# One level of Strassen's multiplication for the input projection of a short convolution, in token passes of 768, 768 and 640

## What is computed

```python
proj = rmsnorm(x, g) @ w_in                    # 2176 x 1024 times 1024 x 4096
b_gate, c_gate, h, z = split(proj, 4)          # four matrices of 1024 columns
u = c_gate * h
conv = w[0]*u[t-2] + w[1]*u[t-1] + w[2]*u[t]   # causal, three taps
y = silu(z) * b_gate * conv
x = x + rmsnorm(y @ w_out)                     # second stage, phase_out
```

## Time and profile before

| | |
|---|---|
| median of 3 runs | 2816.25 us (2815.89 to 2818.65) |
| the profiled execution, own time | 2820.25 us |
| its span in the trace | 2818.7 us |
| first matmul of the projection starts | 22.23 us |
| last matmul of the projection starts | 794.45 us |
| first matmul of phase_out starts | 797.31 us |
| matmuls of the projection | 3840 |
| busy share of PE, DVE, ACT, POOL over the span | 98%, 58%, 47%, 41% |

### The profile page before, as it was taken

How to read it: one execution, slowest core, us unless ns; L and a number is a source line. 1 busy time by engine, 2 the same in 40 slices (tenths; PEclk the granted TensorE clock), 3 DMA queues, 4 the chain that set the end, 5 groups by cost and what they waited for, 6 DMA issues and landing times. The chain is left out here.

```text
span 2818.7 us, 42045 instructions
## 1 busy us (share of the span) xinstructions
PE 2755.2 (98%) x14856; PEld 2409.4 (85%) x14856; DVE 1645.2 (58%) x2152; ACT 1315.5 (47%) x2733; POOL 1156.5 (41%) x1023
## 2 busy tenths in 40 slices
PE   7999999999999999999989999999999999979998
PEld 6999999999978888889978888888888888868886
DVE  5321232123244450102249999999999999998775
ACT  6000000000034441111148888888888888875543
POOL 3333333233210020002356877777777768651110
PEclk9999999999999999999999999999999999999999
DMA  5101110111064444424578676777777866766873
GB/s 160 38 24 38 38 38 22 38 38 38 9 202 131 136 152 153 174 102 157 166 219 269 197 245 198 237 215 217 223 222 207 251 203 207 224 184 203 239 229 107
DMA packets 280359, 433.33 MB, mean 154 GB/s; under 512 B 52578, under 2 KB 218594, under 8 KB 274180
## 3 DMA queue, kind: packets, MB, share of 16 engines
q1 hardware_dynamic: 269156, 391.41, 45.4%
q0 software_dynamic: 11040, 39.86, 4.7%
HBM read 307.40 MB, written 123.81 MB: 153 GB/s over the span
## 5 line engine op out<-in xcount | busy, mean ns | idle before, releaser
L1994 POOL TENSOR_TENSOR a_a<-a_a,a_prod 128x512 f32<-128x512 f32 (+3 forms) x640 | 661.1, 1051 | 270.3 <-DVE a_prod L1945 196.0
L1945 DVE TENSOR_TENSOR_SCAN a_prod<-a_keep,a_prod,a_restart 128x513 f32<-128x513 f32 x384 | 478.0, 1269 | 7.5 <-ACT a_keep L1889 5.7
L1888 ACT ACTIVATE a_a<-a_pz 128x512 f32<-128x512 f32 (+3 forms) x640 | 357.4, 559 | 69.4 <-PE a_pz L1815 44.4
L1955 DVE TENSOR_TENSOR a_atl<-a_pt,a_ath 128x512 fp32r<-128x512 f32 (+3 forms) x640 | 363.0, 599 | 33.0 <-ACT a_ath L1898 29.9
L1889 ACT ACTIVATE a_keep<-a_pz 128x512 f32<-128x512 f32 (+3 forms) x640 | 361.4, 565 | 0.0
L1898 ACT ACTIVATE a_ath<-a_pt 128x512 fp32r<-128x512 f32 (+3 forms) x640 | 333.0, 558 | 57.8 <-PE a_po L1829 34.2
L1838 PEld LDWEIGHTS a_pt<-ident_r,a_bits 128*128 128x128 f32 x2176 | 231.4, 141 | 51.1 <-DVE a_atl L1955 7.4
L285 POOL TENSOR_TENSOR w_wh<-w_raw,w_gain 128x1024 fp32r<-128x1024 f32 x22 | 41.7, 1897 | 534.2 <-PE v_pg L355 278.9
L1814 PE MATMUL a_pz<-a_kh,a_q 128*128 128x512 f32 (+3 forms) x640 | 246.9, 389 | 8.7 <-ACT a_keep L1889 6.2
L1827 PE MATMUL a_po<-a_ath,a_v 128*128 128x512 f32 (+3 forms) x640 | 250.8, 396 | 2.7 <-POOL a_v L2005 1.9
L1838 PE MATMUL a_pt<-ident_r,a_bits 128*128 128x128 f32 x2176 | 244.2, 241 | 6.4 <-DVE a_atl L1955 4.2
(11 more groups left out here) (234 smaller groups left out, 6128.0 us busy)
## 6 DMA issues: line engine op xcount, KB each, us to landing
a_x<-x_d SPq DMA_DIRECT2D x84, 896.0 KB, 6.7
a_x<-x_d SPq DMA_DIRECT2D x56, 832.0 KB, 5.9
a_kh<-kh_t SPq DMA_DIRECT2D x32, 512.0 KB, 6.9
a_kl<-kl_t SPq DMA_DIRECT2D x32, 512.0 KB, 8.8
w_raw<-in_a_w_in POOLq DMA_DIRECT2D x30, 512.0 KB, 4.8
x<-f_xn POOLq DMA_DIRECT2D x17, 512.0 KB, 5.9
g_y_in<-sz_t SPq DMA_DIRECT2D x17, 512.0 KB, 7.9
g_x<-x SPq DMA_DIRECT2D x17, 512.0 KB, 3.6
```

The costliest lines, as they stand in the source:

```text
L1888: act.activation(a[:, s, q, 0:w], pz[:, n % ZS, 0:w], ACT.Sigmoid, scale=SCALE)
L1945: dve.tensor_tensor_scan(prod[:, s, 0:w + 1][:, ::-1], keep[:, n % KS, 0:w + 1][:, ::-1], restart[:, 0:1].broadcast_to([P, w + 1]), prod[: ...
L1955: dve.tensor_tensor(atl[:, b % AS, c0:], pt[:, turn_slot(pr, hh, b), c0:], ath[:, b % AS, c0:].bitcast(F32), ALU.subtract).then_inc(at_spl ...
L1994: pool.tensor_tensor(part, part, prod[:, n % PS, after:after + w], ALU.mult).then_inc(weighted, 1)
```

## The change

Tokens go in three passes of 768, 768 and 640 (`PASSES` gives start and half width: 384, 384, 320). A strip is (pass, c, pair of matrices), 48 in all. Even strips (m = 0) make c_gate and h of one column c, odd strips (m = 1) z and b_gate. Within a strip the weights are a 2 x 2 block matrix A (which matrix x which half of the 1024 inputs) and x is a 2 x 2 block matrix B (which half of the inputs x which half of the pass's tokens). Seven products of 4 x 3 matmuls take the place of eight. Sums of weights S1 to S4 are made by POOL for each strip, differences of x T1 to T4 once a pass. Each of the seven weight operands is split by ACT (high) and DVE (low) anew for every strip, and each of the seven x operands once a pass. The gain is folded into x when DVE reads the transposes (`stage`). Norm and transposes of the tiles of passes 1 and 2 are spread over the strips of the pass before. Three PSUM banks a strip, two sets: bank A takes A11*B11 and, once ACT has copied it, A12*B21; bank B takes S1*T1 and S4*B22; bank C takes S2*T2, S3*T3 and A22*T4. DVE adds the partial results (v, u2, c12, c22, c21). Products with the gates move from DVE to POOL, the first tap and the carry of two tokens between passes move to ACT, the other taps stay with DVE. `phase_norm_in` goes; its work is in `phase_conv`. In phase_out, 5 of the 8 row blocks of w_out are split ahead of the barrier (4 high and 2 low before), and two scratch tiles lie elsewhere.

```diff
+PASSES = [(0, 384), (768, 384), (1536, 320)]
+STRIPS = [(p, c, m) for p in range(NPASS) for c in range(KT) for m in range(2)]
+FIRST_TILES = 2 * PASSES[0][1] // P
...
+            def product(n, i):                       # TensorE
+                w, fresh = width(n), i in (A11_B11, S1_T1, S2_T2)
...
+                elif i == A12_B21:
+                    pe.wait_ge(p1_read, n + 1)
+                elif i == S4_B22:
+                    pe.wait_ge(v_read, n + 1)
+                elif i == S3_T3:
+                    pe.wait_ge(u2_read, n + 1)
+                elif i == A22_T4:
+                    pe.wait_ge(c22_read, n + 1)
+                if first_of_pass(n):
+                    pe.wait_ge(x_lo[i], p + 1)
+                pe.wait_ge(w_lo[i], n + 1)
+                o = bank(n, b, w)
+                for k in range(NH):
+                    x_h, x_l = room.xh[i][:, k, 0:w], room.xl[i][:, k, 0:w]
+                    pe.matmul(o, room.wh[i][:, k, :], x_h, start=fresh and k == 0, ...)
+                    pe.matmul(o, room.wh[i][:, k, :], x_l, start=False, ...)
+                    mm = pe.matmul(o, room.wl[i][:, k, :], x_h, start=False, ...)
+            for t in range(FIRST_TILES):
+                turn(t)
+            for n in range(NSTRIP):
+                if n >= 2 and n - 2 in norm_of:
+                    turn(norm_of[n - 2])
...
+                product(n, A11_B11)
+                product(n, S1_T1)
+                if n:
+                    product(n - 1, A22_T4)
+                product(n, S2_T2)
+                product(n, A12_B21)
+                product(n, S4_B22)
+                product(n, S3_T3)
...
+            for n in range(NSTRIP):                  # ScalarE
+                act.wait_ge(done[A11_B11], n + 1)
+                act.activation(room.p1[:, n % 2, 0:w], bank(n, BANK_A, w), ACT.Copy).then_inc(p1_read, 1)
+                high(n + 1, A11_B11)
+                if m == 0 and n:
+                    open_gate(n - 1)
+                if m == 0:
+                    prefix(n)
+                high(n + 1, S1_T1)
+                high(n, A22_T4)
+                if m == 1:
+                    keep_and_tap(n)
+                high(n + 1, S2_T2)
+                act.wait_ge(done[A12_B21], n + 1)
...
+                high(n + 1, A12_B21)
+                high(n + 1, S4_B22)
+                high(n + 1, S3_T3)
+                if n in norm_of:
+                    sums_of(norm_of[n])
+                if n - 1 in norm_of:
+                    scale(norm_of[n - 1])
...
+            for n in range(NSTRIP):                  # VectorE
+                if n:
+                    c22(n - 1)
+                    low(n, S3_T3)
+                low(n + 1, A11_B11)
...
+                add(room.v[:, 0:w], n, BANK_B, room.p1[:, n % 2, 0:w], v_read)
+                low(n + 1, S1_T1)
+                if n:
+                    c21(n - 1)
+                low(n, A22_T4)
...
+                add(room.u2[:, 0:w], n, BANK_C, room.p1[:, n % 2, 0:w], u2_read)
+                low(n + 1, S2_T2)
+                if n % 2:
+                    taps(n)
+                low(n + 1, A12_B21)
+                if n - 2 in norm_of:
+                    stage(norm_of[n - 2])
...
+                    add(room.cg[:, w:2 * w], n, BANK_B, room.u2[:, 0:w], c12_read)
...
+                low(n + 1, S4_B22)
...
+            sums(0)                                  # GpSimd
+            first_differences(0)
+            third_difference(0)
+            for n in range(NSTRIP + 1):
+                if n and n % 2:
+                    set_u(n - 1, 1)
+                if n + 1 < NSTRIP:
+                    sums(n + 1)
+                if n and n % 2 == 0:
+                    gate(n - 1, 0)
+                    gate(n - 1, 1)
+                    finish(n - 1, 1)
+                if n % PER_PASS == PER_PASS - 2 and n < PER_PASS * (NPASS - 1):
+                    first_differences(n // PER_PASS + 1)
+                if n % PER_PASS == PER_PASS - 1 and n < PER_PASS * (NPASS - 1):
+                    second_difference(n // PER_PASS + 1)
+                if n and n % 2:
+                    set_u(n - 1, 0)
+                elif n:
+                    finish(n - 1, 0)
+                if n % PER_PASS == PER_PASS - 1 and n < PER_PASS * (NPASS - 1):
+                    third_difference(n // PER_PASS + 1)
```

More of the change, by code:

```diff
@@ L109, in make_tools @@
     return sb, pb, sem, sem2
[L112 to L256, removed]
@@ L361 @@
 EDGES_AT, BORDER_SIZE = 34336, 38432
[L362 removed]
+AHEAD = 5
 class Border:
@@ L428, in phase_conv @@
[L428 to L436 removed]
+        pc = pb("c_pc", [P, 6, 512])
@@ new lines, in phase_conv @@
+        t_set = sem2("c_t_set", 4)
+        raw_loaded = [sem2(f"c_raw_loaded_{x}") for x in "xy"]
+        summed = sem("c_summed")
+        w_hi, w_lo, x_hi, x_lo, done = sem7("w_hi"), sem7("w_lo"), sem7("x_hi"), sem7("x_lo"), sem7("done")
+        p1_read, c11_read, v_read, u2_read, c12_read, c22_read, c21_read = (
+            sem("c_read_" + n) for n in ("p1", "c11", "v", "u2", "c12", "c22", "c21"))
+        opened, prefixed, u_set, tapped, kept, gated = (
+            sem("c_" + n) for n in ("opened", "prefixed", "u_set", "tapped", "kept", "gated"))
@@ new lines, in phase_conv, with bank, width, first_of_pass @@
+        tail = SEQ - PASSES[-1][0]
+        def bank(n, b, w):
+            return pc[:, 3 * (n % 2) + b, 0:w]
+        def width(n):
+            return PASSES[STRIPS[n][0]][1]
+        def first_of_pass(n):
+            return n % PER_PASS == 0
+        def tiles_staged(p):
+            return 2 * (sum(tokens_of(p)[::2]) // P)
+        def pair(n):
+            return n // 2
+        def turned_at(t):
+            if t < FIRST_TILES and t % 2:
+                return pc[:, 4:6, :].rearrange("p b (k f) -> p (b k) f", f=P)
+            return pt[:, :, :]
@@ new lines, in _ @@
+            act.wait_ge(eps_set, 1)
+            act.activation(room.std[:, 0:1], epsb[:, :], ACT.Sqrt).then_inc(warm, 1)
+            act.wait_ge(warm, 1)
+            for t in range(FIRST_TILES):
+                sums_of(t)
+                if t:
+                    scale(t - 1)
+                if t == 3:
+                    high_w(0, A11_B11)
+                elif t == 4:
+                    high_x(0, A11_B11)
+            scale(FIRST_TILES - 1)
+            high_w(0, S1_T1)
+            high_x(0, S1_T1)
@@ L511, in _ @@
+            open_gate(LAST)
             act.wait_ge(e_turned, 1)
+            for i in (A11_B11, A12_B21, A22_T4):
+                act.wait_ge(w_lo[i], LAST)
+            act.wait_ge(summed, 4 * LAST)
             for half in range(2):
[L513 to L516 removed]
@@ L576, in begin_next, with inverse, stage @@
-            def begin_next(g):
-                if g == 1:
+            def inverse(t):
+                dve.wait_ge(std_ready, t + 1)
+                dve.reciprocal(room.rstd[:, t:t + 1], room.std[:, t:t + 1]).then_inc(rstd_ready, 1)
+            def stage(t):
+                p = next(p for p in range(NPASS) if t * P < sum(tokens_of(p)[::2]))
+                at = t * P - PASSES[p][0]
+                dve.wait_ge(turned, t + 1)
+                if t == 0:
+                    dve.wait_ge(gain_loaded, 16)
+                for h in range(2):
+                    half = slice(NH * h, NH * (h + 1))
+                    dve.tensor_tensor(room.stage[:, half, at:at + P], turned_at(t)[:, half, :],
+                                      gain[:, half].unsqueeze(2).broadcast_to([P, NH, P]), ALU.mult).then_inc(staged, 1)
@@ new lines, in add, with c22, c21 @@
+            def add(out, n, b, other, read):
+                w = width(n)
+                dve.tensor_tensor(out, bank(n, b, w), other, ALU.add).then_inc(read, 1)
+            def c22(n):
+                w = width(n)
+                dve.wait_ge(done[S3_T3], n + 1)
+                wait_past(dve, u_set if n % 2 else y_done, 2 * pair(n) + (1 if n % 2 else -1))
+                dve.wait_ge(v_read, n + 1)
+                add(room.sums[:, 1, 0:w], n, BANK_C, room.v[:, 0:w], c22_read)
+            def c21(n):
+                w = width(n)
+                dve.wait_ge(done[A22_T4], n + 1)
+                wait_past(dve, u_set if n % 2 else y_done, 2 * (pair(n) + n % 2))
+                add(room.sums[:, 0, 0:w], n, BANK_C, room.p1[:, n % 2, 0:w], c21_read)
@@ L580, in begin_next @@
                                       ALU.subtract).then_inc(border.y_lo, 1)
-                elif 2 <= g < 2 + LOW_AHEAD:
-                    border.low_weights(dve, range(g - 2, g - 1))
-            with dve.Fori(0, KT - 1) as c:
-                conv_and_gate(c)
-            conv_and_gate(KT - 1)
+                k = n - PER_PASS * (NPASS - 1) - 7
+                if 0 <= k < AHEAD:
+                    border.low_weights(dve, range(k, k + 1))
+            c22(LAST)
+            c21(LAST)
+        @block.gpsimd
```

645 lines of the change are left out of this document (449 added, 196 removed).

## The result

| | before | after |
|---|---|---|
| median | 2817.45 us, 4 runs (2815.89 to 2821.12) | 2859.02 us, 4 runs (2855.14 to 2862.51) |
| span of the profiled execution | 2818.7 | 2860.8 |
| first matmul of the projection starts | 22.23 | 25.6 |
| last matmul of the projection starts | 794.45 | 830.80 |
| first matmul of phase_out starts | 797.31 | 834.78 |

The ratio is 1.0145, with a 95% interval of 1.0128 to 1.0163: slower by 1.5%. The forecast was 2803 with a range up to 2855.

The account below looks back on a forecast made before the run. PE's matmul pace bounds the projection: 657.5 + 9.7 + 5 + 25 + 38 + 45 + 1.5 = 781.7 us against 794.6, 13 less, so a median of 2803 from 2816.25; range 2750 to 2855.

Parts of the forecast that it names:

- Eleven tiles' transposes stand between products, 0.64 a tile, with the switch 0.73: 8.0: Projection, on PE: eleven tiles' transposes between products add 8.0 us by their own duration and the switch.
- the whole term of 9.7: Work added on PE in the projection: 8.0 us for tile transposes, 1.7 for transposes of stream state and edges.
- 2 us of half pace, in the start: Start of the projection: 2 us for matmuls at half pace after idle, counted within the 45 us of start.
- c22 in passes 0 and 1: Steady strips of 384 columns: PE just doesn't wait for DVE's c22; 5 us in all for 16 pairs, 0 to 35.
- c22 late in every odd strip: Slower rival, 27%: POOL's set_u, ACT's keep_and_tap and DVE's S2 operand delay c22; 2874 us, half way 2840.
- sign for that rival: Passes 0 and 1: the slower case shows if PE waits over 1 us in each pair.
- Last pass and steps: PE's waits: 25 us in the last pass (5 to 54), 38 at the two steps between passes (25 to 50).
- 26.4 in 24.0: Last pass: operations of POOL and DVE that take turns need 26.4 us in a pair of strips of 24.0.
- a walk through the order of the queues: Last pass: following the engines' operations ends c22 at 17.6 to 18.7, needed at 15.5; 21 us over 8 pairs.
- The rival in which they cost as much as 384 columns: Matmuls of 320 columns: if the weight load sets 0.173 us each, 40 us more, 2843; chance 5%.
- Start: Start of the projection: 45 us beyond the products, against 36 before; between 37 and 50.
- turns as the forecast took them: A DVE operation with two SBUF inputs and a POOL operation take turns, each whole; one that waited costs 0.15 less.

Follow-up runs that it names:

- turn_late: Changed kernel with each tile's transposes moved from the strip's head to behind product A22*T4 of the strip before: 2824.16 us, ratio 1.0014 to the kernel before.
- keep_clock: Changed kernel with 22 transposes of the identity on PE ahead of the wait for the scaled tile: 2838.11 us, ratio 1.0069 to the kernel before.
- one_x: Changed kernel without the x operands of passes 1 and 2, the products using those of pass 0: 2819.51 us in one execution.
- u_mid: u_ahead with POOL's first half of u, in the last pass, between its second and third sum of the next strip: 2800.41 us, ratio 0.9932.
- u_ahead: turn_late plus DVE's taps in even strips, u2_first's order, and POOL's u product ahead of the second difference in strips 14 and 30: 2811.63 us, ratio 0.9971.
- u2_first: turn_late with DVE making u2 before the operands of A22*T4 in the first strip of each pass: 2822.15 us, ratio 1.0013.

## Why the prediction was wrong

**The step that failed: "Eleven tiles' transposes stand between products, 0.64 a tile, with the switch 0.73: 8.0".** It counts the instructions that PE gained and not what they wait for; for the wait the sum has nothing, and gives no reason. The transposes wait for ACT's scaling, the scaling stands behind the high part of the next S3 operand, and that waits for the end of the product just before the transposes. This can be read from the order of the calls in the changed kernel: PE waits at least for ACT's two operations, which take 0.54 and 1.13. The wait measured 1.76 each, 1.93 from start to start, 21.2 in all, with 11.7 of half pace behind it. turn_late shows it: without these waits the kernel is 35 us faster, 1.45% of slowdown becomes 0.14%, and the forecast's sum would have been off by 13 us instead of 50. The price of the transposes themselves was nearly right: the whole term of 9.7 measured 11.5.

**The second: the clock.** The forecast allowed 2 us of half pace, in the start. Yet a row showed it: 0.42 a matmul behind a wait of 2.52. The waits of PE that the forecast did count, 5, 25 and 38 us, carried none of it. It measured 36.7 us beside 95 us of waits. keep_clock shows that it is a cost of its own.

**c22 in passes 0 and 1: right, and better than taken.** 5 was the term, 0 was measured away from the step between them, also in turn_late, where no other wait can cover it. The rival "c22 late in every odd strip", whose times of 2840 to 2874 hold the measured one, is therefore not what happened: the time fell into its range by another cause. The forecast's sign for that rival was a wait of over 1 us in each pair of the first two passes. PE waited so in 13 of the 16: in eleven for the tile, in the two at the steps for u2 and c22.

**Last pass and steps: the waits were sized well.** 25 forecast and 25.3 measured, 38 and 31.3; the half pace, 10.8 and 6.0, comes on top. For the steps the work on the x operands is the reason, as forecast (one_x). For the last pass the forecast gave two reasons, the sum "26.4 in 24.0" and a walk through the order of the queues, and the trace bears out the walk. This is strip 41 of the changed kernel, ahead of a wait for c22; POOL, ACT, DVE, then PE:

```profile
734.91 0.89 POOL L865 TENSOR_TENSOR c_u<-c_sums,c_cg 128x320 f32<-128x320 f32 x1
```

```profile
735.82 0.20 ACT L592 ACTIVATE c_edge<-c_u 128x2 f32<-128x2 f32 x1 [4.40 <-POOL c_u L865]
```

```profile
737.60 0.69 DVE L699 TENSOR_TENSOR c_wl<-c_s,c_wh 128x512 fp32r<-128x512 f32 x1 [3.40 <-ACT c_wh L554]
```

```profile
745.51 0.64 PE L474 MATMUL c_pc<-c_xh,c_wh 128*128 128x320 f32 x1 [5.71 <-DVE c_sums L706]
```

DVE stands idle for 3.40 us in the strip whose c22 comes 5.71 too late: it waits for ACT, and ACT for the half of u that POOL makes behind four sums. So it isn't DVE's time that is short there, and u_mid, with all the work, wins 10 us by order alone. That the 25 of the forecast met the 25.3 doesn't show the sum of turns to be right.

**Matmuls.** 384 columns are 0.1733 as in the earlier trace rows. 320 columns are 0.1463 where 0.143 was taken, 0.002 above the higher of its two bounds; with it the matmuls are 4.9 us more. The rival in which they cost as much as 384 columns fell. These lines give 0.145 to 0.146 a start:

```profile
829.35 0.31 PE L475 MATMUL c_pc<-c_xl,c_wh 128*128 128x320 f32 x1
829.49 0.30 PE L476 MATMUL c_pc<-c_xh,c_wl 128*128 128x320 f32 x1
...
830.80 0.31 PE L476 MATMUL c_pc<-c_xh,c_wl 128*128 128x320 f32 x1
```

**Start.** 45 forecast and 50.7 measured, 5.7 more; the half pace in it is 8.2 where 2 was forecast. S1*T1 began at 36.29 where its operand was forecast for 30.0, and S3*T3, the later limit, at 57.30 where 55.6 was forecast.

**What stays open.** From the last matmul of the projection to the end of the span the kernel before takes 2024.2 us and the changed one 2030.0, a seventh of the 42 us by which the span is longer. 1.1 of the 5.8 is the step into phase_out, 0.4 is phase_out. The attention, in which nothing is changed, is 5.2 longer (from its first to its last matmul into a_pz 1068.6 us before and 1073.8 after), and what comes behind it 0.9 shorter. The variants, with the same instructions behind the projection, take 2023.7 (keep_clock) to 2030.2 (u_ahead), and in the attention 1069.7 and 1075.3. The ten executions of turn_late alone lie 5.8 us apart. So this looks like scatter; no run was made to settle it. Why the clock fell behind seven of the eleven equal waits and not behind the other four is open too.

## What to carry to other kernels

An instruction put into a full engine's stream costs its duration and its wait: follow its semaphore back through the order of the engine that releases it, and if that engine first waits for the product just ahead, the wait can't be hidden and the instruction belongs a product or two later. Where PE waits, allow for half-pace matmuls behind the wait, here 0.1 to 3.6 us behind each and 37 us beside 95 of waits in all. When two engines take turns, how full they are tells only where to look for a wait. What decides it shows in the order of their queues: here the place of one product of 1 us in POOL's queue was worth 10 us.

## What the runs showed of the hardware

*The clock fell behind short waits.* Behind seven of eleven waits of 1.76 us came 10 to 12 matmuls 0.32 apart instead of 0.174. Behind the other four, of the same length, only one was late, by 0.1. What decides between the two, no run here tells.

*A POOL operation can be kept out by several DVE operations in a row, but needn't be.* POOL's third difference at the start of the changed kernel, then DVE:

```profile
40.86 8.40 POOL L845 TENSOR_TENSOR c_stage<-c_stage 128x1536 f32<-128x1536 f32 x1 [6.84 <-DVE c_xl L692]
```

```profile
40.70 0.68 DVE L699 TENSOR_TENSOR c_wl<-c_s,c_wh 128x512 fp32r<-128x512 f32 x1
41.30 1.75 DVE L692 TENSOR_TENSOR c_xl<-c_stage,c_xh 128x1536 fp32r<-128x1536 f32 x1
42.97 0.68 DVE L699 TENSOR_TENSOR c_wl<-c_s,c_wh 128x512 fp32r<-128x512 f32 x1
43.57 1.75 DVE L692 TENSOR_TENSOR c_xl<-c_stage,c_xh 128x1536 fp32r<-128x1536 f32 x1
45.24 0.68 DVE L699 TENSOR_TENSOR c_wl<-c_raw,c_wh 128x512 fp32r<-128x512 f32 x1
45.84 0.55 DVE L706 TENSOR_TENSOR c_v<-c_pc,c_p 128x384 f32<-128x384 f32 x1
```

It lasts 8.40 where the one at 295.48 in u_ahead lasts 3.43. DVE's last operation with two SBUF inputs ends at 45.9, and POOL ends 3.3 later: as far as the records show, it got nothing done in 5 us, beside five DVE operations of which none lasted over 1.75. The same place in turn_late, whose instructions are the same up to here, POOL and then DVE:

```profile
40.52 3.87 POOL L845 TENSOR_TENSOR c_stage<-c_stage 128x1536 f32<-128x1536 f32 x1 [6.84 <-DVE c_xl L692]
```

```profile
40.97 5.04 DVE L692 TENSOR_TENSOR c_xl<-c_stage,c_xh 128x1536 fp32r<-128x1536 f32 x1
```

Here POOL got in behind the first DVE operation, and DVE's next one waited for it. In the profiled executions of the changed kernel, keep_clock and u2_first POOL was kept out (8.4 us), in those of the other seven variants it was not (3.9), and in all ten it came 0.15 to 0.16 us behind the start of the same DVE operation. So turns as the forecast took them, one operation each, are what the runs show mostly and not always; no other POOL operation of the stage in the changed kernel has two DVE operations on SBUF alone within it. The Trainium skill ("SBUF — State Buffer", Who interferes with whom) calls the shared ports an exclusive lock, says that a DVE instruction with two SBUF inputs contends with a GpSimd instruction that reads SBUF, and that issue order decides who blocks. The traces agree that whole operations wait; which engine gets in next, the order of issue doesn't settle here.
